# Two row blocks of the scores in one visit of TensorE, and a new order of the fill work

## The chip, the cores and the metric

The kernel runs on one core of a Trainium2 chip. The metric is the device time of one execution in microseconds (us); the kernel before was timed three times, and the median counts. The granted TensorE clock is 1.00 (2.4 GHz) throughout the profiled execution.

## The reference, cut to what matters

One decoder layer over 512 tokens and a width of 1024, in float32:

- RMS norm, then one input projection into two head groups: eight heads of block-sparse attention (MoBA) and four heads of differential attention, which have two maps of 64 dimensions and one value of 128.
- In both groups q and k get an RMS norm per head and rotary positions. With 512 tokens and MoBA blocks of 256 keys every past block is chosen, so MoBA attention is plain causal attention here.
- Differential attention subtracts lambda times the second softmax map from the first, multiplies by v, and norms each head's output.
- The output projection is added to the input; an RMS norm and a SwiGLU feed-forward part (hidden width 2816) follow, with another residual.

Attention is therefore, for every head and every query row, `softmax(mask(q k^T / 8)) v` over the causal keys.

## The kernel before

**Number format.** Large products are made of three TensorE matmuls in float32r: each operand is split into a rounded part ("hi", by ScalarE) and the remainder ("lo", by VectorE), and hi x hi, hi x lo and lo x hi are accumulated (lines 1473 to 1475 in the helper `product`). Small products (scores, transposes, mean squares, probabilities times v) are plain float32.

**Pairs.** Attention is worked through in eight pairs of maps: pairs 0 to 3 are MoBA (two heads each), pairs 4 to 7 differential (one head with its two maps each). A map takes 64 of the 128 partitions. For each pair three projections (q, k, v) of 8 steps each are needed, 24 "fills" of three matmuls; fill n of pair p+1 is issued between the attention steps of pair p, so that TensorE has work while VectorE and ScalarE handle the softmax of pair p. In pair 7 the fills are steps of the output projection. The first four fills of pair 1 come before the first scores.

**One pair on TensorE.** `scores(t, qt)`, qt = 0 to 3, multiplies the 128 queries of row block qt with the (qt+1) x 128 causal keys, for both maps, into PSUM banks 2 and 3. `turn_v` transposes v (bank 7). `turn_p(t, qt)` transposes the normed probabilities into banks 4 and 5. `mean_squares(t+1)` and `spread_k(t+1)` serve the norms of the next pair. `heads_out` multiplies with v in bank 6. `turn_o(t-1)` transposes the normed output of a differential head. The next scores need `k_ready`, which VectorE writes once `spread_k` is done.

**One row block on the other engines.** `maxima`: VectorE adds the mask to the diagonal block in PSUM (line 1011), takes the row maxima (1014) and makes the bias (1017). `exps`: ScalarE takes the exponentials of both maps with their sums (622). `norm`: VectorE inverts the sums (1027) and scales the probabilities of a MoBA pair (1030, 1031), or makes the factor of the second map (1033) and combines the maps (1036). `pt_copy`: ScalarE copies the transposed probabilities (632). Scores of row block qt+1 overwrite banks 2 and 3 and wait for the exponentials of block qt.

**Next pair's preparation.** ScalarE evacuates q, k and v (`q_evac`, `k_evac`, `v_evac`, lines 593, 596, 608). SP's queue rotates q and k by DMA (four of 64 KB each) and, between them, issues the loads of weight tiles (512 KB each). VectorE applies rotary positions (`q_rope`, `k_rope`, 974 to 978), computes the scales with eleven small dependent operations (`scales`, 919 to 929), spreads k's scale (965) and writes `k_ready` (1002). `project_hi` (ScalarE, 549) and `project_lo` (VectorE, 936) split weight tiles.

**A bank shared by q and v.** The projections of q and v go to bank 0, that of k to bank 1. The first fill of a pair's q therefore waits until v of the pair before has been copied out; v's copy waits for the last of the 24 fills:

```python
if j == 0 and from_(p, 1):
    pe.wait_ge(v_ev, p)
```

**What sets the order.** The order on every engine is written out by hand, in the texts of ScalarE (lines 676 to 757), VectorE (1107 to 1197) and TensorE (1655 to 1777), with separate texts for pair 0, pairs 1 to 3, pair 4, pairs 5 and 6, and pair 7. An engine takes its instructions in that order, and semaphores hold it where data aren't ready. After a differential pair, `o_squares`, `o_norm`, `turn_o`, `mix_hi` and `mix_lo` norm its output, during the pair that follows.

Of the kernel before, what the change touches and what calls it, by code (L numbers as in the profile page):

```python
# [58 lines left out]
WARM = 4  # L59

# [71 lines left out]
def build(nc, x, wt, vec, gain2, lams, ident_in, mask_in, cos_in, sin_in, out):  # L132
    with ExitStack() as ctx:
# [211 lines left out]

        def maps(moba):

            return range(2) if moba else range(1)
# [196 lines left out]
        def _(act):  # L545
# [64 lines left out]
            def exps(t, qt, moba):  # L610

                W = (qt + 1) * P
                act.wait_ge(nb_s, t * 4 + (qt + 1))
                for a in range(2):
                    i = 2 * qt + a

                    if qt >= 2:
                        act.wait_ge(pt_s, turned(t, qt - 2, a, moba))
                    elif from_(t, 1):
                        moba_before = t - 1 < MOBA_PAIRS if isinstance(t, int) else moba  # L620
                        act.wait_ge(pt_s, turned(t - 1, qt + 2, a, moba_before))
                    nc.scalar.activation(PR[qt % 2][:, a, 0:W], ps[:, 2 + a, 0:W], ACT.Exp, bias=NB[:, i:i + 1],  # L622
                                         scale=RQ[:, i:i + 1], accum_out=SUM[:, i:i + 1]).then_inc(ex_s, 1)

            def pt_copy(t, qt, moba):

                for a in maps(moba):
                    act.wait_ge(pt_s, turned(t, qt, a, moba))
                    if from_(t, 1):
                        act.wait_ge(pv_s, t)  # L630
                    bank = 4 + (a if moba else qt % 2)
                    nc.scalar.activation(PT[:, a, 0:qt + 1, qt * P:(qt + 1) * P],
                                         ps[:, bank, 0:(qt + 1) * P].rearrange("p (k q) -> p k q", q=P),
                                         ACT.Copy).then_inc(pt_ev, 1)
# [40 lines left out]

            exps(0, 0, True)
            project_hi(1, 2)
            exps(0, 1, True)
            pt_copy(0, 0, True)
            q_evac(1, False)  # L680
            pt_copy(0, 1, True)
            exps(0, 2, True)
            project_hi(1, 3)
            k_evac(1, False)
            exps(0, 3, True)
            pt_copy(0, 2, True)
            pt_copy(0, 3, True)
            v_evac(1)
            project_hi(1, 4)
            mix_hi(0, True)  # L690

            with act.Fori(1, MOBA_PAIRS) as t:
# [12 lines left out]
                project_hi(t + 1, 4)  # L705
                v_evac(t + 1)
                mix_hi(t, True)
# [4 lines left out]
            exps(4, 1, False)  # L712
            exps(4, 2, False)
            project_hi(5, 3)
            q_evac(5, False)
            pt_copy(4, 1, False)
            exps(4, 3, False)
            k_evac(5, False)
            pt_copy(4, 2, False)
            pt_copy(4, 3, False)  # L720
# [3 lines left out]
            with act.Fori(MOBA_PAIRS + 1, PAIRS - 1) as t:  # L724
                project_hi(t + 1, 2)
                exps(t, 0, False)
                pt_copy(t, 0, False)
                exps(t, 1, False)
                o_squares(t - 1)
                exps(t, 2, False)  # L730
                project_hi(t + 1, 3)
                q_evac(t + 1, True)
                pt_copy(t, 1, False)
                exps(t, 3, False)
                k_evac(t + 1, True)
                pt_copy(t, 2, False)
                mix_hi(t - 1, False)
                pt_copy(t, 3, False)
                project_hi(t + 1, 4)
                v_evac(t + 1)  # L740
# [3 lines left out]
            exps(7, 0, False)  # L744
            exps(7, 1, False)
            pt_copy(7, 0, False)
            exps(7, 2, False)
# [3 lines left out]
            exps(7, 3, False)  # L751
# [155 lines left out]
        def _(dve):  # L907
# [72 lines left out]
            def q_rope(p):  # L980
                if from_(p, 1):
                    dve.wait_ge(sc_s, p * 4)
# [14 lines left out]
            def k_norm(p):  # L997
                dve.wait_ge(kb_s, p + 1)
                dve.wait_ge(k_step, p * 3 + 3)
                if from_(p, 1):  # L1000
                    dve.wait_ge(sc_s, p * 4)
                nc.vector.tensor_tensor(KF[:], KS[:], ps[:, 7], ALU.mult).then_inc(kn_s, 1)

            def maxima(t, qt):

                W = (qt + 1) * P
                n = t * 4 + (qt + 1)
                i = slice(2 * qt, 2 * qt + 2)
                diagonal = ps[:, 2:4, qt * P:W]
# [4 lines left out]
                nc.vector.tensor_reduce(MX[:, i], ps[:, 2:4, 0:W], AX.X, ALU.max).then_inc(mx_s, 1)  # L1014
# [5 lines left out]
            def norm(t, qt, moba):  # L1020


                W = (qt + 1) * P
                i = 2 * qt
                p0, p1 = PR[qt % 2][:, 0, 0:W], PR[qt % 2][:, 1, 0:W]
                dve.wait_ge(ex_s, t * 8 + (i + 2))
                nc.vector.reciprocal(RS[:, i:i + 2], SUM[:, i:i + 2]).then_inc(rs_s, 1)
                dve.wait_ge(rs_s, t * 4 + (qt + 1))
                if moba:
                    nc.vector.tensor_scalar(p0, p0, RS[:, i:i + 1], None, ALU.mult).then_inc(pn_s, 1)  # L1030
                    nc.vector.tensor_scalar(p1, p1, RS[:, i + 1:i + 2], None, ALU.mult).then_inc(pn_s, 1)
                else:
                    nc.vector.scalar_tensor_tensor(out=NL[:, qt:qt + 1], in0=SUM[:, i:i + 1], scalar=MLAM,
                                                   in1=RS[:, i + 1:i + 2], op0=ALU.mult, op1=ALU.mult).then_inc(lr_s, 1)
                    dve.wait_ge(lr_s, t * 4 + (qt + 1 - 4 * MOBA_PAIRS))
                    nc.vector.scalar_tensor_tensor(out=p0, in0=p1, scalar=NL[:, qt:qt + 1], in1=p0,
                                                   op0=ALU.mult, op1=ALU.add).then_inc(pn_s, 1)
                    if qt == TT - 1:
                        sums = SUM.rearrange("p (t a) -> p t a", a=2)[:, :, 0]
                        nc.vector.scalar_tensor_tensor(out=EO, in0=sums, scalar=EPS, in1=sums, op0=ALU.mult,  # L1040
                                                       op1=ALU.mult).then_inc(eo_s, 1)
# [65 lines left out]
            maxima(0, 0)  # L1107
            norm(0, 0, True)
            maxima(0, 1)
            v_scale(0)  # L1110
            norm(0, 1, True)
            maxima(0, 2)
            project_lo(1, 2)
            norm(0, 2, True)
            maxima(0, 3)
            project_lo(1, 3)
            norm(0, 3, True)
# [7 lines left out]
            with dve.Fori(1, MOBA_PAIRS) as t:  # L1125
                maxima(t, 0)
                norm(t, 0, True)
                maxima(t, 1)
                v_scale(t)
                norm(t, 1, True)  # L1130
                maxima(t, 2)
                project_lo(t + 1, 2)
                norm(t, 2, True)
                maxima(t, 3)
                project_lo(t + 1, 3)
                norm(t, 3, True)
                q_rope(t + 1)
                scales(t + 1)
                k_rope(t + 1)
                k_norm(t + 1)  # L1140
                project_lo(t + 1, 4)
                mix_lo(t, True)

            maxima(4, 0)
            norm(4, 0, False)
# [837 lines left out]
```

## Time and profile before

| | us |
|---|---|
| median of three runs | 622.77 (622.37 to 623.19) |
| span of the profiled execution, first to last instruction | 619.5 |
| TensorE busy | 600.8 |
| VectorE busy | 483.7 |
| ScalarE busy | 311.4 |
| pairs 0 to 7, first scores to the end of the last heads | 36.52 to 255.30 |

For the profiled execution the profile gives the span; what lies around the span has no figure of its own there and is read from the median of the runs, 3.3 us above it. Matmuls overlap in their pipeline: one of 512 columns is shown with 0.39 us, and the next one starts 0.23 us after it. The start times are what counts for TensorE's pace. Idle time of an engine other than TensorE costs nothing unless TensorE waits for its result.

### The profile page before, as it was taken

Reading aid. Unit: us, or ns where it says so; the run is one execution under the profiler, and the core shown is the slowest. Engines: PE = TensorE matmul, PEld = TensorE weight load, DVE = VectorE, ACT = ScalarE, POOL = GpSimd, SP = SyncE. Lnnn points to the kernel's source line nnn. Section 1 sums busy time; section 2 is a strip of 40 time slices with the busy share of each in tenths; the row PEclk is TensorE's granted clock in tenths of the full one; section 3 lists DMA queues with packets and bytes.
Section 4 is the critical chain, followed back from the end, with each engine's and each line's share of the span. In section 5 each row is a group of like instructions: output and inputs, shape, how many; then the busy total and the mean of one; then the engine's idle time right before and its main releaser. Section 6 shows DMA issues by size and latency. Waiting matters only on the chain.

```text
span 619.5 us, 10404 instructions
## 1 busy us (share of the span) xinstructions
PE 600.8 (97%) x3774; PEld 515.5 (83%) x3774; DVE 483.7 (78%) x821; ACT 311.4 (50%) x533; POOL 28.1 (5%) x28
## 2 busy tenths in 40 slices
PE   5999999999999889999999999999999999999997
PEld 5867677776777576878999999999999998888886
DVE  3867777787687888678878787788778877999774
ACT  5445546364545454445653644445444555555551
POOL 0000000000000000000000000000000012145200
PEclk9999999999999999999999999999999999999999
DMA  8324040322314051512413422333213449699901
GB/s 306 92 70 129 1 136 17 119 59 77 102 35 137 0 169 68 170 36 95 178 35 136 137 71 85 119 136 130 75 69 136 136 125 260 196 190 204 198 35 68
DMA packets 32953, 70.31 MB, mean 114 GB/s; under 512 B 3344, under 2 KB 3728, under 8 KB 32912
## 3 DMA queue, kind: packets, MB, share of 16 engines
q1 hardware_dynamic: 26896, 58.22, 28.0%
q0 software_dynamic: 6016, 11.54, 10.6%
q8 instruction: 27, 0.44, 0.3%
q14 instruction: 14, 0.11, 0.1%
HBM read 63.45 MB, written 2.10 MB: 106 GB/s over the span
## 4 chain that ended last, share of the span: by engine, by line
PE 87%; DVE 7%; issue 2%; ACT 2%; DMA 1%; SPq 0%; DVEq 0%; ACTq 0%
PE ps L1473 26%; PE ps L1474 25%; PE ps L1475 25%; PE ps L1537 3%; PE ps L1550 2%; PE ps L1505 2%; PE ps L1567 1%; DMA w_raw<-wt 1%; DVE w_lo L954 1%; ACT probs L622 1%; PE ps L1575 1%; DVE w_lo L936 1%; PE ps L1796 1%; DVE residual L1205 0%; DVE small L1014 0%
## 5 line engine op out<-in xcount | busy, mean ns | idle before, releaser
L1473 PE MATMUL ps<-h_sum_parts,w_hi 128*128 128x256 f32 x432 | 120.6, 279 | 0.7 <-ACT q_kept L806 0.7
L1474 PE MATMUL ps<-h_sum_parts,w_hi 128*128 128x256 f32 x432 | 120.9, 280 | 0.0
L1475 PE MATMUL ps<-h_sum_parts,w_lo 128*128 128x256 f32 x432 | 120.5, 279 | 0.0
L1473 PE MATMUL ps<-h_parts,w_hi 128*128 128x512 f32 x192 | 81.2, 423 | 2.7 <-DVE h_parts L1071 2.4
L1473 PEld LDWEIGHTS ps<-h_sum_parts,w_hi 128*128 128x128 f32 x432 | 81.2, 188 | 0.9 <-ACT q_kept L806 0.9
L1474 PEld LDWEIGHTS ps<-h_sum_parts,w_hi 128*128 128x128 f32 x432 | 81.1, 188 | 0.0
L1475 PEld LDWEIGHTS ps<-h_sum_parts,w_lo 128*128 128x128 f32 x432 | 80.8, 187 | 0.0
L1475 PE MATMUL ps<-h_parts,w_lo 128*128 128x512 f32 x192 | 75.4, 393 | 0.0
L1474 PE MATMUL ps<-h_parts,w_hi 128*128 128x512 f32 x192 | 75.0, 391 | 0.0
L622 ACT ACTIVATE probs<-ps,small 128x128 f32<-128x128 f32 (+3 forms) x64 | 39.0, 614 | 51.8 <-DVE small L1017 51.8
L1473 PE MATMUL ps<-w_hi,hidden_parts 128*128 128x512 f32 x154 | 59.9, 389 | 0.0
L1475 PE MATMUL ps<-w_hi,hidden_parts 128*128 128x512 f32 x154 | 59.9, 389 | 0.0
L1474 PE MATMUL ps<-w_lo,hidden_parts 128*128 128x512 f32 x154 | 59.9, 389 | 0.0
L1474 PE MATMUL ps<-h_first_parts,w_hi 128*128 128x256 f32 x192 | 53.8, 280 | 0.0
L1473 PE MATMUL ps<-h_first_parts,w_hi 128*128 128x256 f32 x192 | 53.7, 280 | 0.0
L1475 PE MATMUL ps<-h_first_parts,w_lo 128*128 128x256 f32 x192 | 53.6, 279 | 0.0
L1473 PEld LDWEIGHTS ps<-h_parts,w_hi 128*128 128x128 f32 x192 | 36.2, 189 | 19.8 <-issue 13.7
L954 DVE TENSOR_TENSOR w_lo<-w_raw,w_hi 128x1024 fp32r<-128x1024 f32 x29 | 35.3, 1222 | 16.4 <-ACT w_hi L584 16.4
L1475 PEld LDWEIGHTS ps<-h_parts,w_lo 128*128 128x128 f32 x192 | 36.0, 188 | 8.2
L954 DVE TENSOR_TENSOR w_lo<-w_raw_odd,w_hi 128x1024 fp32r<-128x1024 f32 x25 | 30.5, 1221 | 13.2 <-ACT w_hi L584 13.2
L1474 PEld LDWEIGHTS ps<-h_parts,w_hi 128*128 128x128 f32 x192 | 36.2, 189 | 5.3
L529 POOL DMA_DIRECT2D w_raw_odd<-wt x12 | 14.6, 1214 | 541.3 <-DVE w_lo L1313 541.3
(175 smaller groups left out, 1248.7 us busy)
## 6 DMA issues: line engine op xcount, KB each, us to landing
w_raw<-wt SPq DMA_DIRECT2D x61, 512.0 KB, 4.2
w_raw_odd<-wt SPq DMA_DIRECT2D x24, 512.0 KB, 4.2
w_raw_odd<-wt POOLq DMA_DIRECT2D x12, 512.0 KB, 7.8
down_raw<-wt SPq DMA_DIRECT2D x6, 512.0 KB, 11.0
w_raw<-wt POOLq DMA_DIRECT2D x5, 512.0 KB, 10.2
residual<-x SPq DMA_DIRECT2D x4, 512.0 KB, 5.1
q_rotated<-q_gained SPq DMA_DIRECT2D x32, 64.0 KB, 2.0
k_rotated<-k_gained SPq DMA_DIRECT2D x32, 64.0 KB, 2.0
```

The lines of the kernel that those rows point to most:

```text
L529: pool.dma_start(down_raw("B11", c).rearrange("p (f n) -> p f n", n=SEQ), down_rows(role, c), accum_op=ALU.add).then_inc(tb_added[c], 16)
L622: nc.scalar.activation(PR[qt % 2][:, a, 0:W], ps[:, 2 + a, 0:W], ACT.Exp, bias=NB[:, i:i + 1], scale=RQ[:, i:i + 1], accum_out=SUM[:, i:i ...
L936: nc.vector.tensor_tensor(WL[:, slot], RAW[:, slot], WH[:, slot].bitcast(F32), ALU.subtract).then_inc(w_lo, 1)
L954: nc.vector.tensor_tensor(WL[:, n % SLOTS], product_source(n), WH[:, n % SLOTS].bitcast(F32), ALU.subtract).then_inc(c_lo, 1)
L1473: nc.tensor.matmul(dst, lh, rh, start=start, stop=False, skip_group_check=True)
L1474: nc.tensor.matmul(dst, lh, rl, start=False, stop=False, skip_group_check=True)
L1475: return nc.tensor.matmul(dst, ll, rh, start=False, stop=stop, skip_group_check=True)
L1505: ins = nc.tensor.matmul(ps[:, 7, c:c + 2], SQ[:, tt * P:(tt + 1) * P], IND, start=True, stop=True, skip_group_check=True)
L1537: ins = nc.tensor.matmul(ps[:, 2 + a, 0:W], QF[rows[a], qs], KF[rows[a], 0:W], start=True, stop=True, skip_group_check=True)
L1550: ins = nc.tensor.transpose(ps[:, bank, kt * P:(kt + 1) * P], PR[qt % 2][:, a, kt * P:(kt + 1) * P], ident[:])
L1567: ins = nc.tensor.matmul(ps[rows, 6, qs], VF[:, kt, rows], PT[:, a, kt, qs], start=kt == 0, stop=kt == TT - 1, skip_group_check=True)
L1575: ins = nc.tensor.matmul(ps[:, 6, qs], PT[:, 0, kt, qs], VF[:, kt], start=kt == 0, stop=kt == qt, skip_group_check=True)
```

## The change

Row blocks 0 and 1 become one visit: `VISITS = ((0, 1), (2,), (3,))`. TensorE writes the scores of block 1 (256 wide) at columns 0 to 255 of banks 2 and 3 and those of block 0 at columns 256 to 383, four matmul calls with one semaphore step. VectorE adds the mask to both diagonal blocks, which lie side by side, in one operation, takes two sets of maxima, and makes one bias for all four; ScalarE takes four exponentials; VectorE inverts four sums at once. The transposed probabilities of block 0 in a MoBA pair go to the last quarter of banks 4 and 5, so that blocks 0 and 1 can be turned one right after the other. `pt_copy` of block 0 in a MoBA pair waits for the turn of block 1.

The order of all three engines is new in every pair. On TensorE, with the fills as numbers (S scores, T turn_p, TV turn_v, TO turn_o, MS mean_squares, H0 and H1 heads_out, SK spread_k; the indices are row blocks):

```
pairs 1-3 before: 1 S0 2 TV 1 S1 T0 4 S2 4 T1 S3 6 T2 MS T3 5 H0 SK 1 H1
pairs 1-3 after:  1 S01 2 TV 4 S2 1 T0 T1 3 S3 T2 6 T3 MS 4 H0 SK H1 3
pair 0 before:    4 S0 TV 2 S1 3 T0 1 S2 1 T1 4 S3 2 T2 5 T3 MS 2 H0 SK H1
pair 0 after:     4 S01 2 TV 4 S2 1 T0 T1 3 S3 T2 3 T3 MS 4 H0 SK H1 3
pair 5, 6 before: 1 S0 1 TV 1 S1 T0 4 S2 4 T1 1 S3 1 TO 5 T2 1 MS T3 5 H0 SK H1
pair 5, 6 after:  1 S01 2 TV 4 S2 1 T0 T1 3 S3 2 T2 TO 4 T3 MS 4 H0 SK H1 3
pair 7 before:    TV 1 S0 3 S1 3 S2 2 T0 T1 2 S3 TO 5 T2 2 T3 3 H0 H1
pair 7 after:     S01 TV 5 S2 2 T0 T1 3 S3 3 T2 TO 4 T3 4 H0 H1
```

Pair 4 after is as pairs 5 and 6 without TO. The core of the diff, in which visit 1 is row block 2 and visit 2 is row block 3:

```diff
+VISITS = ((0, 1), (2,), (3,))
+NV = len(VISITS)
+def score_at(qt):
+    return 2 * P if qt == 0 else 0
...
-            def scores(t, qt):
+            def scores(t, v):
...
-                for a in range(2):
-                    ins = nc.tensor.matmul(ps[:, 2 + a, 0:W], QF[rows[a], qs], KF[rows[a], 0:W], start=True,
-                                           stop=True, skip_group_check=True)
+                for qt in VISITS[v]:
+                    W = (qt + 1) * P
+                    at = score_at(qt)
+                    for a in range(2):
+                        ins = nc.tensor.matmul(ps[:, 2 + a, at:at + W], QF[rows[a], qt * P:W], KF[rows[a], 0:W],
+                                               start=True, stop=True, skip_group_check=True)
                 ins.then_inc(sc_s, 1)
...
+                at = P if v == 0 else first * P
+                diagonal = ps[:, 2:4, at:at + blocks * P].rearrange("p a (b k) -> p a b k", b=blocks)
                 dve.wait_ge(sc_s, n)
-                nc.vector.tensor_tensor(diagonal, diagonal, mask[:].unsqueeze(1).broadcast_to([P, 2, P]),
+                nc.vector.tensor_tensor(diagonal, diagonal,
+                                        mask[:].unsqueeze(1).unsqueeze(1).broadcast_to([P, 2, blocks, P]),
                                         ALU.add).then_inc(masked, 1)
...
             def pt_copy(t, qt, moba):
...
-                    act.wait_ge(pt_s, turned(t, qt, a, moba))
+                    act.wait_ge(pt_s, turned(t, max(qt, 1) if moba else qt, a, moba))
...
             with act.Fori(1, MOBA_PAIRS) as t:
+                project_hi(t + 1, 2)
                 exps(t, 0, True)
                 pt_copy(t, 0, True)
                 exps(t, 1, True)
-                project_hi(t + 1, 2)
+                pt_copy(t, 1, True)
+                q_evac(t + 1, False)
                 project_hi(t + 1, 3)
                 exps(t, 2, True)
-                pt_copy(t, 1, True)
-                q_evac(t + 1, False)
-                exps(t, 3, True)
+                pt_copy(t, 2, True)
                 k_evac(t + 1, False)
-                pt_copy(t, 2, True)
                 pt_copy(t, 3, True)
                 project_hi(t + 1, 4)
+                mix_hi(t, True)
                 v_evac(t + 1)
-                mix_hi(t, True)
...
             with dve.Fori(MOBA_PAIRS + 1, PAIRS - 1) as t:
                 maxima(t, 0)
+                v_scale(t)
+                project_lo(t + 1, 2)
                 norm(t, 0, False)
                 maxima(t, 1)
-                v_scale(t)
-                project_lo(t + 1, 2)
+                o_norm(t - 1)
                 norm(t, 1, False)
                 maxima(t, 2)
-                o_norm(t - 1)
-                maxima(t, 3)
+                mix_lo(t - 1, False)
                 norm(t, 2, False)
-                norm(t, 3, False)
-                mix_lo(t - 1, False)
-                project_lo(t + 1, 3)
                 q_rope(t + 1)
                 scales(t + 1)
                 k_rope(t + 1)
+                project_lo(t + 1, 3)
                 k_norm(t + 1)
                 project_lo(t + 1, 4)
```

In pairs 5 and 6 ScalarE takes `o_squares(t - 1)` ahead of the first exponentials, and `q_evac` and `mix_hi(t - 1)` ahead of the last. In pair 7 ScalarE takes `out_hi` and `mix_hi(6)` ahead of the last exponentials, as before, and VectorE takes `o_norm(6)` between the second maxima and their norm. In the MoBA pairs VectorE takes `project_lo(t + 1, 4)` ahead of `k_norm(t + 1)`.

## Rows read from the trace of the kernel before

**Rows 1.** the page, busy time, share of the span and instructions.

```profile
PE 600.8 (97%) x3774; PEld 515.5 (83%) x3774; DVE 483.7 (78%) x821; ACT 311.4 (50%) x533; POOL 28.1 (5%) x28
```

**Rows 2.** busy time by stretch, from scores to scores; stretch, length, busy (instructions).

```profile
36.52:64.22 27.70, 26.07 (x141) 18.21 (x140) 20.14 (x49) 14.14 (x33) 0.00 (x0) 1.00 0.26 77
...
92.15:120.02 27.87, 27.87 (x150) 19.91 (x149) 20.64 (x49) 14.45 (x33) 0.00 (x0) 1.00 0.24 75
...
147.88:174.67 26.79, 26.33 (x144) 20.17 (x143) 20.37 (x50) 13.32 (x29) 0.00 (x0) 1.00 0.26 79
174.67:203.28 28.61, 27.05 (x147) 20.60 (x147) 22.80 (x63) 14.17 (x37) 0.00 (x0) 1.00 0.24 75
203.28:255.30 52.02, 49.08 (x261) 36.92 (x261) 41.97 (x107) 26.43 (x70) 0.00 (x0) 1.00 0.24 82
```

**Rows 3.** waits of TensorE from 36 to 256 us; total, times, longest.

```profile
PE ps L1537 <- ACT probs L622: 2.1, 5, 0.6
PE ps L1537 <- DVE k_ready L1002: 2.0, 2, 1.3
PE ps L1522 <- DVE k_ready L1002: 1.3, 1, 1.3
PE ps L1513 <- DVE k_rstd_spread L965: 0.5, 2, 0.3
PE ps L1550 <- DVE probs L1036: 0.4, 2, 0.2
```

**Rows 4.** TensorE's timeline, pair 2; start, length of the group, instructions.

```profile
92.15 0.49 PE L1537 MATMUL ps<-k_ready,q_ready 64*128 64x128 f32 x4
...
95.30 0.70 PE L1537 MATMUL ps<-k_ready,q_ready 64*128 64x256 f32 x4
...
103.31 1.13 PE L1537 MATMUL ps<-k_ready,q_ready 64*128 64x512 f32 x4
104.36 0.50 PE L1473 MATMUL ps<-h_parts,w_hi 128*128 128x512 f32 x1
104.70 0.39 PE L1474 MATMUL ps<-h_parts,w_hi 128*128 128x512 f32 x1
...
108.33 0.39 PE L1475 MATMUL ps<-h_parts,w_lo 128*128 128x512 f32 x1
```

**Rows 5.** TensorE's weight loads at the same 512-wide scores.

```profile
103.30 0.30 PEld L1537 LDWEIGHTS ps<-k_ready,q_ready 64*128 64x128 f32 x4 [0.17 <-ACT probs L622]
```

**Rows 6.** TensorE's timeline before pair 0, first fill of pair 1.

```profile
32.44 0.39 PE L1475 MATMUL ps<-h_parts,w_lo 128*128 128x512 f32 x1
...
33.61 0.47 PE L1473 MATMUL ps<-h_parts,w_hi 128*128 128x512 f32 x1 [0.34 <-ACT v_by_dim L608]
```

**Rows 7.** ScalarE's timeline, v's copy there; exponentials in pair 2.

```profile
32.87 0.60 ACT L608 ACTIVATE v_by_dim<-ps 128x512 f32<-128x512 f32 x1 [6.12 <-PE ps L1475]
...
94.14 0.46 ACT L622 ACTIVATE probs<-ps,small 128x128 f32<-128x128 f32 x1 [2.10 <-DVE small L1017]
...
97.51 0.56 ACT L622 ACTIVATE probs<-ps,small 128x256 f32<-128x256 f32 x1 [0.77 <-DVE small L1017]
```

**Rows 8.** VectorE's timeline, pair 2.

```profile
97.32 0.69 DVE L994 TENSOR_TENSOR v_turned<-ps,small 128x512 f32<-128x512 f32 x1
...
104.48 0.43 DVE L1011 TENSOR_TENSOR ps<-ps,mask 128x256 f32<-128x256 f32 x1 [0.42 <-PE ps L1537]
...
108.07 0.17 DVE L1027 RECIPROCAL small<-small 128x2 f32<-128x2 f32 x1 [0.53 <-ACT probs L622]
108.27 0.49 DVE L1030 TENSOR_SCALAR probs<-probs,small 128x512 f32<-128x512 f32 x1
```

**Rows 9.** VectorE's timeline, pair 5, output's norm and last combining.

```profile
184.08 0.16 DVE L921 SCALAR_TENSOR_TENSOR small<-small 128x4 f32<-128x4 f32 x1
...
186.48 0.69 DVE L1047 TENSOR_TENSOR o_normed<-ps,small 128x512 f32<-128x512 f32 x1
...
191.43 0.75 DVE L1036 SCALAR_TENSOR_TENSOR probs<-probs,small 128x512 f32<-128x512 f32 x1
```

More of the change, by code:

```diff
@@ L344, in turned, with turned_at @@
             return t * 4 + (4 * MOBA_PAIRS + qt + 1)
+        def turned_at(qt, moba):
+            return 3 * P if moba and qt == 0 else 0
         def maps(moba):
@@ L1018, in maxima @@
                                                op1=ALU.mult).then_inc(nb_s, 1)
[L1020 to L1041, printed above, removed]
@@ new lines, in norm @@
+            def norm(t, v, moba):
+                first, blocks = VISITS[v][0], len(VISITS[v])
+                i, last = 2 * first, 2 * (first + blocks)
+                dve.wait_ge(ex_s, t * 8 + last)
+                nc.vector.reciprocal(RS[:, i:last], SUM[:, i:last]).then_inc(rs_s, 1)
+                dve.wait_ge(rs_s, t * NV + (v + 1))
+                if not moba:
+                    nc.vector.scalar_tensor_tensor(out=NL[:, first:first + blocks], in0=SUM[:, i:last:2], scalar=MLAM,
+                                                   in1=RS[:, i + 1:last:2], op0=ALU.mult,
+                                                   op1=ALU.mult).then_inc(lr_s, 1)
+                    dve.wait_ge(lr_s, t * NV + (v + 1 - NV * MOBA_PAIRS))
+                for qt in VISITS[v]:
+                    W = (qt + 1) * P
+                    p0, p1 = PR[qt % 2][:, 0, 0:W], PR[qt % 2][:, 1, 0:W]
+                    if moba:
+                        nc.vector.tensor_scalar(p0, p0, RS[:, 2 * qt:2 * qt + 1], None, ALU.mult).then_inc(pn_s, 1)
+                        nc.vector.tensor_scalar(p1, p1, RS[:, 2 * qt + 1:2 * qt + 2], None,
+                                                ALU.mult).then_inc(pn_s, 1)
+                    else:
+                        nc.vector.scalar_tensor_tensor(out=p0, in0=p1, scalar=NL[:, qt:qt + 1], in1=p0, op0=ALU.mult,
+                                                       op1=ALU.add).then_inc(pn_s, 1)
+                if not moba and v == NV - 1:
+                    sums = SUM.rearrange("p (t a) -> p t a", a=2)[:, :, 0]
+                    nc.vector.scalar_tensor_tensor(out=EO, in0=sums, scalar=EPS, in1=sums, op0=ALU.mult,
+                                                   op1=ALU.mult).then_inc(eo_s, 1)
@@ L1107, in _ @@
             maxima(0, 0)
+            v_scale(0)
+            project_lo(1, 2)
             norm(0, 0, True)
             maxima(0, 1)
-            v_scale(0)
             norm(0, 1, True)
             maxima(0, 2)
-            project_lo(1, 2)
+            project_lo(1, 3)
             norm(0, 2, True)
-            maxima(0, 3)
-            project_lo(1, 3)
-            norm(0, 3, True)
             q_rope(1)
@@ L1157, in _ @@
             k_rope(5)
+            project_lo(5, 3)
             k_norm(5)
@@ L1177, in _ @@
                 k_rope(t + 1)
+                project_lo(t + 1, 3)
                 k_norm(t + 1)
@@ L1678, in _ @@
             heads_out(0, 1, True)
+            fill(3)
             with pe.Fori(1, MOBA_PAIRS) as t:
@@ L1727, in _ @@
             heads_out(4, 1, False)
+            fill(3)
             with pe.Fori(MOBA_PAIRS + 1, PAIRS - 1) as t:
@@ L1754, in _ @@
                 heads_out(t, 1, False)
+                fill(3)
             fill = out_filler()
+            scores(7, 0)
             turn_v(7)
-            fill(1)
-            scores(7, 0)
-            fill(3)
+            fill(5)
             scores(7, 1)
-            fill(3)
-            scores(7, 2)
             fill(2)
@@ L1766, in _ @@
             turn_p(7, 1, False)
-            fill(2)
-            scores(7, 3)
+            fill(3)
+            scores(7, 2)
+            fill(3)
+            turn_p(7, 2, False)
             turn_o(6)
-            fill(5)
-            turn_p(7, 2, False)
-            fill(2)
+            fill(4)
             turn_p(7, 3, False)
-            fill(3)
+            fill(4)
             heads_out(7, 0, False)
```

228 lines of the change are left out of this document (107 added, 121 removed).

## The prediction

> **What bounds the kernel now.** I read the page's busy times first. TensorE is busy 97% of the span [rows 1]: whatever the other engines save is worth only what it takes out of TensorE's waits. The stage table, cut at the first scores of each pair, says where there are any [rows 2]: pairs 1 to 3 have TensorE busy for their whole 27.9 us (pair 2 stands for them), pair 0 lacks 1.6 us, pair 4 0.5, pair 5 1.6, pairs 6 and 7 together 2.9. The waits of TensorE between 36 and 256 us add to 6.3 us, 2.1 of them on exponentials, 3.3 on k_ready, 0.5 on the k spread, 0.4 on normed probabilities [rows 3]. Start to start, against the pace of undisturbed neighbours, the same 15 stalls cost 8.0 us, since the pipeline also drains: 1.8 in pair 0, 0.6 in pair 4, 2.0 in pair 5, 3.7 in pairs 6 and 7. That is all the change can win from waits.
>
> The other reserve is the order of the stream itself. The 72 fill matmuls of a pair go at 0.227 to 0.229 us each (16 steps between the second and the eighteenth after the last scores take 3.63 us [rows 4]), 16.5 us in all. Every group of f32 work between them costs its own length, about 0.1 us ahead of it when it is scores or heads and 0.08 to 0.11 behind it (0.34 from 104.36 to 104.70 against 0.23 [rows 4]). What is left of pair 2's 27.87 [rows 2], 11.36 us, is the cost of its groups.
>
> **What the change removes from TensorE's stream.** No matmul goes away. Scores take, start to next start, 0.42, 0.63 and 1.06 us at 128, 256 and 512 wide (their rows less 0.07 us of tail [rows 4]): 0.21, plus 0.21 for every 128 columns, both heads side by side. The merged visit is 0.42 + 0.63 = 1.05 us if its halves only follow each other, 0.85 if the second has no 0.21 of its own; I take 0.95, as the weights of the second pass are loaded while the first runs (4 loads in 0.30 us at the head of a visit of 1.06 [rows 4, 5]), and keep 0.85 and 1.05 as bounds. One pair of edges (0.20) goes. The Trainium skill, "TensorE: Matmul & The Clock Gate", part 3 "The mechanism", says that a weight load overlaps matmuls in flight only where the row groups differ; the merged visit comes back to row group 0, so by that rule it is 1.05 and the sum 0.8 us higher. The trace is against the strict reading, by that row of loads, but shows no second visit behind a first.
> The other groups, start to next start in pairs 0 and 2 of TensorE's timeline less the fills' own pace: a turn appended to scores costs 0.09 us a transpose and no edge; turns of row blocks 0 and 1 together, six transposes like turn 2 of pair 0, 0.66; turn 3 and the mean squares 2.66; heads, k spread, heads in one piece 3.24. So a MoBA pair's groups cost 11.0 us, 0.37 less than now; pair 0 saves 0.36, pair 4 0.21, pairs 5 and 6 0.28 each, pair 7 0.4. Together -2.7 us.
>
> **What it adds: the wait for v_by_dim.** Now heads (and in MoBA pairs one fill) stand between the last v product of a pair and the first fill of the next, which writes the same bank 0 and waits for ScalarE's copy of v. After, each pair ends with three fills and the loop begins with fill(1), so nothing stands between them. The trace has this wait once with only a short k spread inside: last matmul 32.44, copy 32.87 for 0.60, next fill 33.61 [rows 6, 7]. That is 1.17 us instead of 0.23, plus 0.08 behind it: 1.0 us (0.9 to 1.05 with the spread of such wake-ups). Behind it on TensorE queue the fill, then the scores, so the whole stream moves. It comes at six pair ends, 0 to 5 (pair 6 is followed by scores, not by a fill): +6.0 us. Its cover today is the 0.8 us of heads; now mixed_parts covers nothing of it, being released before the three fills.
>
> **The new schedule, from the start of the merged scores (0).** VectorE: mask from 1.07; 512 elements per partition in PSUM step 0.61 (the v scaling, 0.69 with its overlap [rows 8]) to 0.86 (two masks of 0.43), I take 0.7; maxima 0.4 and 0.7; bias out at 3.1. ScalarE from 3.2: 0.45 + 0.45 + 0.56 + 0.69 (the rows for 128 and 256 wide, the last with its reading of the sum and the way to TensorE [rows 7]), so the second scores may start at 5.35. TensorE arrives there after fill 2, turn v, fill 4 at 5.70: margin 0.35, no wait. The project_lo and v scaling now between maxima and norm lie beside the exponentials (end 4.9, norm from 5.33): free. Turn 0 at 7.3 finds its probabilities (6.6). Second scores end 6.55, bias 8.1, exponentials 8.33 to 9.8; ScalarE's first copies of turned probabilities, which now wait for turn 1 too, end 8.3, just in time. Third scores arrive at 10.1 in MoBA pairs (margin 0.3), at 9.83 in differential ones (margin 0.04).
> The last step is where margin runs out. From the start of the 512-wide scores to their first normed map is 5.45 us and 0.1 to TensorE (103.31; mask 104.48; exponentials; reciprocal 108.07; scaling 108.27 for 0.49 [rows 4, 8]). Pairs 1 to 3 put turn 2 and six fills between (5.8 us): hidden. Pair 0 puts three (3.8): +1.7 us. Differential pairs put two fills, turn 2 and four fills: 5.65, against 6.0 with their extra small scale (0.25) and a combining operation of 0.75 instead of 0.49 [rows 9]: pair 4 +0.4. In pairs 5 and 6 the output's norm now sits between the second maxima and norm 1: 2.2 us of small steps and 0.6 (184.08 to 186.48 with a hiccup of 0.2, then the product [rows 9]); maxima 2 start at 12.1 instead of 11.0 and turn 3 finds its map at 17.0 where TensorE is at 15.85: +1.1 each. Pair 7: no fill before turn v and five behind it, so the second scores wait 0.4; turn 3 is ready 17.8, as ScalarE must first take mixed_parts behind turn o, against 16.9: +0.9; the fill that needs w_out_parts 0.1. Together +1.7 +0.4 +2.2 +1.4 = +5.7 us.
> DMAs: the moved evacuations issue the q and k rotations and the weight loads behind them on SP's queue. q is evacuated at 11.6 and needed at 16.6, k at 16.8 and needed at 22.0, loads are needed 5 us or more after their issue: hidden. k_ready, which ends 1.5 to 3 us before the scores that want it, stops being a wait even behind the project_lo now ahead of it in MoBA pairs; what is late next is v_by_dim, in every pair. After pair 7 the stream of w_out is TensorE's and moves one for one.
>
> **The sum.** Waits removed -8.0, groups -2.7, v_by_dim +6.0, new waits +5.7: +1.0 us. Walking the same schedule start by start gives +0.4 (pair 0 +0.4, pairs 1 to 3 +0.5 each, pair 4 +0.6, pair 5 -0.1, pairs 6 and 7 -1.95; the lower value of each edge taken). I take +0.8. The profiled execution spans 619.5 us, and 3.3 us lie between that and the median of 622.77; the change touches nothing outside the span, so 620.3 and **623.5**. Bounds: merged scores 0.1 each way in 8 pairs, 0.8; v wait -0.6 to +0.3; the waits behind the third scores 0.2 each in five pairs, 1.0. These hardly all fall together: 622.0 to 625.0.
>
> **Rivals.**
> (a) *The first chain binds everywhere.* Slower. Second scores have 0.35 us of margin behind mask, two maxima, bias and four exponentials. If the merged mask with its two broadcast axes costs 0.86, 0.16 goes; should the four-dimensional access be slower still, or the exponentials queue behind ScalarE's weight split, which now runs first in the pair, every 0.1 us beyond the margin costs 0.8 us over eight pairs, and the third scores, with 0.04 in differential pairs, follow at once. 0.6 us more of chain: +0.25 x 8 = 2.0, 625.5. For it: thin margins in all pairs. Against: TensorE's chains in the trace repeat within 0.05 us, and the split ends before 0. It decides from 0.35 us.
> (b) *The new waits are at their cheap end.* v copy 0.9, merged scores 0.85, and the last map ready 0.2 sooner five times: -0.6 -0.8 -1.0 = -2.4 from the forecast, 621.1, faster than before. For it: waits of the trace vary by 0.3 between pairs. Against: three terms must lean one way; the v wait is fixed by a copy that lasts 0.60 in all eight pairs.
> (c) *The visit isn't merged in effect.* Second halves wait for the first to drain: 1.05 and edges kept, +0.3 a pair, part swallowed by later waits: +1.5, 625.0. The row of loads is against it.
> A measurement of this kernel tells about 0.2% (1.2 us) from no change. Forecast 0.62 for itself, of which a third of its upper part passes 624.0; (a) 0.13, (b) 0.15, (c) 0.10. Faster by over 0.2% takes most of (b): 0.14. Slower takes (a), (c) and 0.12 of the forecast: 0.34. Same: 0.52. The range takes the forecast's own 622.0 to 625.0 and reaches a little into (a) and (b): 621.7 to 625.2.
>
> **What would show it.** In the changed trace: scores 0.85 to 1.05 from the first matmul of the merged visit to the next fill; no wait on k_ready; a wait of TensorE's fill line on v_by_dim six times, about 0.75 us idle each; waits on normed probabilities in pairs 0, 4, 5, 6 and 7 and none in 1 to 3; MoBA pairs of 28.4 to 28.5 us instead of 27.9; TensorE's busy time some 2 us less by overlap counted. I am wrong if the fill line shows no wait on v_by_dim, if scores wait on exponentials in pairs 1 to 3, or if pairs 6 and 7 together don't fall by 1.5 us or more.

## The result: 0.8% slower, and the profile after

The changed kernel took 627.15 us (median of 6 runs, 624.81 to 628.19) against 622.31 for the kernel before (6 runs, 620.69 to 623.19): ratio 1.0084, 95% interval 1.0069 to 1.0099. The forecast was 623.5 and its range ended at 625.2. The profiled execution took 626.56 us and spans 624.7 us; in the six runs 1.75 to 1.86 us lie outside the span. The kernel before's profiled 619.5 us therefore stood for some 621.3 us.

First the page of the changed kernel: the busy time of TensorE, and the granted clock in 40 slices.

```profile
PE 603.6 (97%) x3774; PEld 518.1 (83%) x3774; DVE 478.3 (77%) x793; ACT 309.3 (50%) x533; POOL 28.1 (4%) x28
...
PEclk9997999999999999999999999999999999999999
```

TensorE is as full as before [rows 1], but one slice, from 47 to 62 us, has a clock of 7 tenths. The kernel before has a 9 in all forty. Next, TensorE's waits of the changed kernel from 36 to 262 us (total, times, longest), which answer to [rows 3].

```profile
PE ps L1485 <- ACT v_by_dim L622: 4.7, 6, 0.8
PE ps L1566 <- DVE probs L1058: 2.8, 4, 0.9
PE ps L1566 <- ACT probsT L649: 1.5, 1, 1.5
PE ps L1550 <- ACT probs L638: 0.2, 1, 0.2
```

k_ready and the k spread are gone from the list, and the three waits named in the forecast stand in it: v_by_dim six times, normed probabilities in pairs 4 to 7 (written at line 1058 of the changed kernel), and the wait of pair 0 before turn 3, 1.5 us, which the trace puts down to ScalarE's copy of the third row block's turned probabilities. VectorE finishes the first normed map at 51.67 us, some 0.06 us before turn 3 starts, so the map that the forecast named was hardly earlier than that copy:

```profile
51.19 0.48 DVE L1054 TENSOR_SCALAR probs<-probs,small 128x512 f32<-128x512 f32 x1
```

Then the stretches of the changed kernel from scores to scores, answering to [rows 2] (stretch, length, busy time of the engines, granted clock, DMA share, GB/s).

```profile
36.15:67.53 31.38, 29.11 (x140) 20.52 (x139) 20.07 (x46) 14.08 (x33) 0.00 (x0) 0.89 0.22 68
...
96.08:124.63 28.55, 27.77 (x149) 19.86 (x149) 19.98 (x46) 14.10 (x33) 0.00 (x0) 1.00 0.24 73
...
153.18:180.58 27.40, 26.39 (x143) 20.05 (x142) 19.52 (x45) 12.40 (x30) 0.00 (x0) 1.00 0.26 77
180.58:210.65 30.07, 28.40 (x147) 21.65 (x147) 22.63 (x58) 13.85 (x38) 0.00 (x0) 0.94 0.24 71
210.65:260.60 49.95, 48.08 (x262) 36.70 (x261) 40.18 (x98) 26.73 (x71) 0.00 (x0) 1.00 0.29 89
```

| pairs | before | walked in the forecast | after | clock after |
|---|---|---|---|---|
| 0 | 27.70 | 28.1 | 31.38 | 0.89 |
| 1 to 3, each | 27.87 to 27.93 | 28.4 | 28.55 | 1.00 |
| 4 | 26.79 | 27.4 | 27.40 | 1.00 |
| 5 | 28.61 | 28.5 | 30.07 | 0.94 |
| 6 and 7 | 52.02 | 50.1 | 49.95 | 1.00 |

Where the clock is 1.00 the walk start by start (the forecast's second way of adding) holds within 0.15 us a pair. The two pairs where it is off, by 3.3 and 1.6 us, are the two with a clock below 1. The same changed kernel in steps of 2 us, around turn 3 of pair 0 and of pair 5:

```profile
50.00:52.00 2.00, 0.51 (x4) 0.27 (x3) 1.40 (x5) 2.00 (x7) 0.00 (x0) 1.00 0.63 135
52.00:54.00 2.00, 2.00 (x19) 2.00 (x17) 1.97 (x4) 1.92 (x5) 0.00 (x0) 0.88 0.53 201
54.00:56.00 2.00, 2.00 (x9) 1.90 (x9) 0.57 (x4) 0.89 (x1) 0.00 (x0) 0.50 0.26 62
56.00:58.00 2.00, 2.00 (x6) 1.52 (x6) 1.73 (x10) 0.00 (x0) 0.00 (x0) 0.50 0.60 139
58.00:60.00 2.00, 2.00 (x7) 1.51 (x5) 1.97 (x6) 0.00 (x0) 0.00 (x0) 0.50 0.99 365
60.00:62.00 2.00, 2.00 (x10) 0.49 (x8) 1.19 (x2) 0.00 (x0) 0.00 (x0) 0.91 0.21 86
...
196.00:198.00 2.00, 1.11 (x8) 0.69 (x7) 1.72 (x5) 1.63 (x5) 0.00 (x0) 1.00 0.47 176
...
200.00:202.00 2.00, 2.00 (x7) 1.57 (x6) 1.66 (x11) 0.66 (x1) 0.00 (x0) 0.57 0.31 74
202.00:204.00 2.00, 2.00 (x7) 1.57 (x6) 1.93 (x6) 0.00 (x0) 0.00 (x0) 0.57 0.80 260
```

0.50 is the lower level, 1.2 GHz. Summed over the rows it lasts 6.8 us in pair 0 and 3.4 us in pair 5, and costs half of that, 5.1 us. Each begins two to three microseconds after the end of a wait for the last map (the rows with 0.51 us busy of 2 and 1.11 of 2 hold these waits), in or behind the mean squares. What the matmuls look like there is in TensorE's timeline of the changed kernel, where the ordinary fills are left out and one slow fill is shown (start, length, instructions).

```profile
47.29 0.88 PE L1566 MATMUL ps<-ident,probs 128*128 128x128 f32 x6
...
51.73 1.09 PE L1566 MATMUL ps<-ident,probs 128*128 128x128 f32 x8 [1.49 <-ACT probsT L649]
52.66 0.95 PE L1517 MATMUL ps<-small,q_squared 128*128 128x2 f32 x8
53.47 1.82 PE L1517 MATMUL ps<-small,k_squared 128*128 128x2 f32 x8
...
56.58 0.63 PE L1485 MATMUL ps<-h_parts,w_hi 128*128 128x512 f32 x1
57.00 0.63 PE L1486 MATMUL ps<-h_parts,w_hi 128*128 128x512 f32 x1
```

The last two start 0.42 us apart instead of 0.23. The runs' own clocks tell the same: 624.81 us at 0.994, 626.4 and 626.6 at 0.991, 627.8, 628.0 and 628.2 at 0.989, 1.6 us for each 3.4 us at 1.2 GHz. At full clock this kernel would take about 621.4 us (an estimate, 626.56 less 5.1; no run of it had full clock). The kernel before, in the runs beside the experiments, takes 620.6 to 622.3 us at 1.00 (mostly under 621.5) and 621.9 to 623.4 at 0.997. So between the two profiled executions, whose spans differ by 5.2 us, the clock takes 5.1 and the schedule of the pairs 0.6; 0.4 comes back ahead of the pairs. Between the medians (4.8 us) it is some 0.7 of schedule and 4 of clock, since the median of the kernel before had one such stretch itself.

### The profile page after: what moved, and what is told of

It is laid out like the page before. It is cut to its first block, busy times and chain, and to the rows that moved or that the text cites. A ratio compares the mean times of both kernels' runs of the same rounds, so it can differ in the third digit from the quotient of the medians.

```text
span 624.7 us, 10337 instructions
## 1 busy us (share of the span) xinstructions
PE 603.6 (97%) x3774; PEld 518.1 (83%) x3774; DVE 478.3 (77%) x793; ACT 309.3 (50%) x533; POOL 28.1 (4%) x28
## 4 chain that ended last, share of the span: by engine, by line
PE 90%; DVE 4%; ACT 3%; issue 1%; DMA 1%; SPq 0%; ACTq 0%
PE ps L1485 27%; PE ps L1487 25%; PE ps L1486 25%; PE ps L1550 4%; PE ps L1517 2%; PE ps L1566 2%; PE ps L1583 2%; PE ps L1591 1%; ACT probs L638 1%; DMA w_raw<-wt 1%; DVE w_lo L966 1%; ACT v_by_dim L622 1%; PE ps L1802 1%; PE ps L1525 1%; DVE small L1030 1%
## 5 line engine op out<-in xcount | busy, mean ns | idle before, releaser
L1485 PE MATMUL ps<-h_parts,w_hi 128*128 128x512 f32 x192 | 82.7, 431 | 7.4 <-ACT v_by_dim L622 5.0
L1487 PE MATMUL ps<-h_parts,w_lo 128*128 128x512 f32 x192 | 76.9, 401 | 0.0
L1486 PE MATMUL ps<-h_parts,w_hi 128*128 128x512 f32 x192 | 76.5, 398 | 0.0
L1485 PEld LDWEIGHTS ps<-h_parts,w_hi 128*128 128x128 f32 x192 | 37.0, 193 | 25.5 <-issue 19.6
L638 ACT ACTIVATE probs<-ps,small 128x128 f32<-128x128 f32 (+3 forms) x64 | 38.9, 615 | 28.1 <-DVE small L1035 28.1
L1486 PEld LDWEIGHTS ps<-h_parts,w_hi 128*128 128x128 f32 x192 | 37.2, 194 | 5.8
```

The source lines that it names most:

```text
L638: nc.scalar.activation(PR[qt % 2][:, a, 0:W], ps[:, 2 + a, at:at + W], ACT.Exp, bias=NB[:, i:i + 1], scale=RQ[:, i:i + 1], accum_out=SUM[: ...
L1485: nc.tensor.matmul(dst, lh, rh, start=start, stop=False, skip_group_check=True)
L1486: nc.tensor.matmul(dst, lh, rl, start=False, stop=False, skip_group_check=True)
L1487: return nc.tensor.matmul(dst, ll, rh, start=False, stop=stop, skip_group_check=True)
```

## The experiments

All runs of one group stood on one chip beside the kernel before, whose medians were 622.24 (first four), 621.35 (second four) and 621.32 (last four). "Stretches" are 3.4 us at 1.2 GHz, estimated from a run's mean clock (half of 3.4 us is 0.27% of 625: 0.997 is one, 0.994 two, 0.991 three, 0.989 four). Where they lie is known for the one profiled run of each kernel only.

**The v waits hidden.** In pairs 0 to 6:

```diff
+fill(3)
 heads_out(t, 0, True)
 spread_k(t + 1)
 heads_out(t, 1, True)
-fill(3)
...
+v_evac(t + 1)
 mix_hi(t, True)
-v_evac(t + 1)
```

> The three fills at each pair's end stand ahead of the heads instead of behind them (pairs 0 to 6), and v is copied ahead of mixed_parts. Theory A (the schedule cost 0.8 us over the kernel before, of it six v waits of 1.0; the rest of the loss is the clock at 1.2 GHz for a stretch in pair 0 and one in pair 5): the v waits go, 5 to 6 us less than the changed kernel, the clock still falls in pair 0; about 621 us. Rival B (the v wait only moves on: the next scores then wait for k_ready, since less stands behind the k spread): 0 to 2 us less, waits on k_ready in its place.

Measured: 619.12 us (5 runs), ratio to before 0.9951 (0.9932 to 0.9970). One run at 0.999 took 615.59, four at 0.994 took 618.7 to 619.5. The profile shows no wait on v_by_dim in the pairs, nor on k_ready in its place: 5.8 us less than the estimate for the changed kernel at full clock (621.4). Rival B is out. The stretches went from three or four in most runs to two in four runs of five. The one profiled had none, though its waits for the last map stand with mean squares right behind (1.49 us in pair 0, 0.87 in pairs 5 and 6): theory A's fall in pair 0 didn't come in this run, and where the others had theirs isn't shown.

**Pair 0 fed.**

```diff
 turn_p(0, 2, True)
-fill(3)
+fill(6)
 turn_p(0, 3, True)
 mean_squares(1)
-fill(4)
+fill(1)
```

> Pair 0 alone: six fills instead of three ahead of turn 3, one instead of four behind the mean squares. Theory A (the clock falls where TensorE has stood waiting for the last map and then goes into transposes and mean squares): no wait, clock 1.00 all through pair 0, pair 0 of 28 us or less instead of 31.4; the changed kernel less 3.3 for the clock and 1 to 1.7 for the wait, some of it returned as a wait on the k spread: 4 us less. Rival C (the clock falls by chance of the chip or by the pattern of the whole pair, not by this wait): 1.7 us less at most, clock still at half in pair 0.

Measured: 623.25 us (10 runs), ratio 1.0021 (1.0004 to 1.0038); one to three stretches. The profile has full clock in pair 0 and the low stretches in pairs 4 and 5 (164 to 172 and 196 to 204 us). That pair 0 is at full clock is as theory A has it, and the median is 3.5 us under the changed kernel's 626.72 (measured again below; forecast 4). But in pair 4 TensorE had waited only 0.23 us for the last map (turn 3 at 164.68) before the clock fell at 167.2: the length of the wait alone doesn't decide.

**Pair 0, mean squares set apart.** The wait stays; `fill(2)` stands between `turn_p(0, 3)` and `mean_squares(1)`, and two behind.

> Pair 0 alone: the wait ahead of turn 3 stays, but two of the four fills that follow the mean squares stand between turn 3 and the mean squares. Theory A1 (wait and thin matmuls behind it together bring the clock down): the clock stays at 1.00, 3.3 us less than the changed kernel. Theory A2 (the 1.5 us of waiting alone brings it down): clock at half as before, time as the changed kernel. If neither the wait nor the thin matmuls matter (rival C): as the changed kernel too, and the run with six fills tells it from A2.

Measured: 624.65 us (8 runs), ratio 1.0039 (1.0022 to 1.0056), one to three stretches (most often two). The profile has the full 1.49 us of waiting in pair 0 and full clock there, low stretches in pairs 5 and 6, where the mean squares still stand right behind waits of 0.9 us. That speaks for A1, for one pair in one profile.

**The kernel before, starved.** In its pair 0 `fill(1)` between turns 2 and 3 and `fill(6)` behind the mean squares, for 5 and 2.

> The kernel before, pair 0 alone: one fill instead of five between turns 2 and 3, six instead of two behind the mean squares, so that TensorE waits some 1.5 us for the last map as in the changed kernel, with no merged visit anywhere. Theory A: the clock falls in pair 0 here too and costs 3.3 us; with the wait of 1.6 and less k_ready wait (-1.3) about 3 to 4 us more than before, 626. Rival C (only the new pattern brings the clock down): clock 1.00, 0 to 0.5 us more than before.

Measured: 622.65 us (10 runs), ratio 1.0021 (1.0003 to 1.0038). TensorE waits 1.46 us before turn 3, mean squares right behind, and the clock in pair 0 stays at 1.00 in the profile (its one low stretch is at 12 to 20 us):

```profile
55.01 1.09 PE L1550 MATMUL ps<-ident,probs 128*128 128x128 f32 x8 [1.46 <-ACT probsT L632]
```

```profile
54.00:58.00 4.00, 2.99 (x26) 2.94 (x27) 3.11 (x7) 2.08 (x6) 0.00 (x0) 1.00 0.65 186
```

Two runs of ten had no stretch, seven had one, one had three. Theory A missed here: a wait and thin matmuls behind it are not always enough.

**All maps fed.** Pair 0 as above, and

```diff
 # pairs 5 and 6 (pairs 4 and 7: fill(4) -> fill(5), one less behind)
 turn_o(t - 1)
-fill(4)
+fill(6)
 turn_p(t, 3, False)
 mean_squares(t + 1)
-fill(4)
+fill(2)
```

> The changed kernel with more fills ahead of turn 3: six instead of three in pair 0, five instead of four in pairs 4 and 7, six instead of four in pairs 5 and 6, and as many fewer behind; the v waits stay. Theory A (time is the schedule's sum plus 1.7 us for each 3.4 us stretch at 1.2 GHz, and such stretches come where TensorE waits for the last map and then goes into the thin mean squares): waits of 4.5 us go and the stretches in pairs 0, 4, 5 and 6 with them: 617 us, clock 1.00 or 0.997. Rival D (the v waits bring the clock down as well): clock still 0.994 to 0.991, 620 us or more.

Measured: 620.22 us (10 runs), ratio 0.9976 (0.9964 to 0.9989): three runs at full clock with 618.6 to 619.3, seven at 0.997. Rival D is out: six waits of 0.8 us stand at the pair ends as before (five put down to v_by_dim, the one behind pair 4 to w_lo), and in the profile the clock holds at all of them. Whether the one stretch of the other seven runs lies in the pairs or at the start (see below) isn't shown. The saving of the schedule is 2.8 us where 4.5 were expected: new waits come up behind the maps, 0.55 us for w_out_parts, 0.35 for the k spread and 0.15 ahead of the scores of pair 7; the other 0.6 or so isn't accounted for.

**Both repairs.** The v waits hidden and all maps fed.

> The fills ahead of turn 3 as in the run with all maps fed, and the last three fills of each pair ahead of the heads, v copied ahead of mixed_parts. Theory A: both savings add, 611 to 612 us at clock 1.00. Rival B (with the fills gone from behind the k spread, k_ready or the k spread is waited for): 613 to 616 us with those waits in the profile.

Measured: 611.80 us (4 runs, 611.66 to 613.30), ratio 0.9850 (0.9830 to 0.9871). This beats both kernels. Its stretches from scores to scores:

```profile
36.27:61.76 25.49, 25.49 (x141) 18.25 (x140) 19.44 (x46) 13.41 (x33) 0.00 (x0) 1.00 0.27 83
89.30:116.84 27.54, 27.54 (x150) 19.95 (x149) 20.07 (x46) 14.09 (x34) 0.00 (x0) 1.00 0.25 76
144.38:170.28 25.90, 25.90 (x143) 20.21 (x142) 19.97 (x46) 13.79 (x34) 0.00 (x0) 1.00 0.23 64
170.28:196.63 26.35, 26.35 (x147) 20.69 (x147) 22.10 (x59) 14.10 (x39) 0.00 (x0) 1.00 0.26 79
196.63:245.90 49.27, 48.08 (x262) 37.06 (x261) 40.86 (x99) 26.32 (x67) 0.00 (x0) 1.00 0.31 100
```

Length and TensorE's busy time are one number in pairs 0 to 5. Together, the merged visit, the new order and the two repairs take 9.2 us out of the pairs against [rows 2]; this run doesn't say how much of it is the merging. Pairs 1 to 3 last 27.54 us instead of 27.9.

**Mean squares apart in all four pairs.** As in pair 0 above, also in pairs 4, 5 and 6. No wait is taken away.

> The changed kernel with two of its fills moved from behind the mean squares to between turn 3 and the mean squares, in pairs 0, 4, 5 and 6; no wait is taken away. Theory A1 (a wait and the thin matmuls close behind it must come together for the clock to fall): schedule time as the changed kernel's at full clock, 621 to 622 us, clock 1.00 or 0.997. Theory A2 (the waits alone do it): clock 0.991 to 0.989 and 626 to 628 us, as the changed kernel.

Measured: 624.09 us (10 runs), ratio 1.0039 (1.0027 to 1.0051); four runs at full clock (622.6 to 623.1), six at 0.997. TensorE's waits over the whole execution, and the steps around pair 0's and pair 5's mean squares:

```profile
PE ps L1485 <- ACT v_by_dim L622: 5.0, 7, 0.8
...
PE ps L1566 <- DVE probs L1058: 2.8, 4, 0.9
...
PE ps L1566 <- ACT probsT L649: 1.5, 1, 1.5
```

```profile
54.00:56.00 2.00, 2.00 (x19) 1.92 (x17) 0.32 (x1) 1.02 (x2) 0.00 (x0) 1.00 0.27 66
...
58.00:60.00 2.00, 2.00 (x14) 0.85 (x12) 1.90 (x7) 0.00 (x0) 0.00 (x0) 1.00 0.96 360
...
200.00:202.00 2.00, 1.99 (x19) 1.80 (x18) 1.83 (x8) 0.00 (x0) 0.00 (x0) 1.00 0.20 76
```

The changed kernel has the same three waits to the tenth over its whole execution (the seventh wait on v_by_dim is ahead of pair 0), and here not one run of ten is below 0.997, where the changed kernel had none of ten above 0.994. This is the clearest of the runs: these waits, with two fills ahead of the mean squares, don't bring the clock down. Theory A1 expected 621 to 622 us at full clock and it is 622.6 to 623.1, some 1.4 over the estimate for the changed kernel: two more edges between fills and mean squares in each of four pairs.

**Both repairs, visits split again.** `VISITS = ((0,), (1,), (2,), (3,))`, with `scores(t, 1)` behind turn v and one fill (three in pair 7).

> The run with both repairs, but with row blocks 0 and 1 as two visits again (one or three fills and the turn of v between them), everything else in the same order. This prices the merging alone: two more edges (0.2 us) and 0.21 us of a visit's start in each pair, 0.4 x 8 = 3.3 us more than with both repairs if the merged halves run side by side; 1.6 us if only the edges count; 0 if the merging never mattered. VectorE and ScalarE have one more mask, bias and reciprocal each pair, and no wait on them is expected.

Measured: 623.50 us (7 runs), ratio 1.0026 (1.0013 to 1.0039); at full clock 621.63, 9.9 more than with both repairs. Expected were 3.3 at most. The order didn't fit four visits: TensorE waits 1.5 us for probabilities, 1.3 for exponentials, 0.6 for k_ready, and 1.6 us in two stalls that the trace puts down to no engine. Only pairs 1 to 3 compare: 28.15 us (93.07 to 121.22) against 27.54, 0.6 more a pair, of which some 0.2 is a later start of the last scores (0.54 us after the fill ahead of them, where 0.32 is usual). The 0.4 that is left agrees with the two halves running side by side. What the merging is worth in the other pairs stays open.

This profile also has a fall that theory A1 doesn't cover. Pair 7 has no mean squares. Its last map is waited for 1.45 us, four transposes follow, then a second wait of 0.55, then fills, and the clock falls at about 253.3 us:

```profile
251.90 0.66 PE L1581 MATMUL ps<-ident,probs 128*128 128x128 f32 x4 [1.45 <-DVE probs L1063]
253.11 0.62 PE L1500 MATMUL ps<-w_out_parts,mixed_parts 128*128 128x512 f32 x1 [0.55 <-DVE w_out_parts L962]
```

**The changed kernel again.**

> The changed kernel once more, beside the others, for how often and where its clock falls. Theory A: 0.994 to 0.989, two to four stretches of 3.4 us at 1.2 GHz, each within 3 us behind a wait for the last map, one of them in pair 0; 621.4 us plus 1.7 for each. Rival C (chance): another number of stretches, at places without such a wait.

Measured: 626.72 us (4 runs), ratio 1.0092 (1.0069 to 1.0115), three or four stretches. Low clock in pairs 0, 5 and 6 (52 to 60, 196 to 204, 228 to 236 us), each behind its wait for the last map.

**Fed in pairs 4 to 7 only.**

> The changed kernel with maps fed in pairs 4 to 7 as in the run with all maps fed, and pair 0 left as it is. Theory A: the stretches of pairs 4 to 6 go, those of pair 0 stay: 618.7 (all maps fed, full clock) plus 1.4 for the wait plus one or two stretches of 1.7, clock 0.997 to 0.994, so 622 to 623.5 us, the low clock in pair 0 alone. Rival C: no clear place.

Measured: 622.81 us (10 runs), ratio 1.0016 (0.9999 to 1.0032); eight runs with two stretches, one with one, one at full clock. The profile has one in pair 0 (52 to 60 us) and one at 12 to 20 us, ahead of all pairs; pairs 4 to 7 are at full clock, as theory A has it.

**The kernel before, dense.** In its pair 0 turn 2 right behind the last scores, then `fill(3)`, turn 3, mean squares, `fill(6)`.

> The kernel before, pair 0 alone: turn 2 right behind the last scores, three fills, the wait for the last map, turn 3, mean squares, six fills, so the thin f32 matmuls stand on both sides of the wait as in the changed kernel; no merged visit. Theory A1 (wait and thin matmuls within a few us bring the clock down, whatever kernel they stand in): a low stretch in pair 0, clock 0.997 to 0.994 over what the kernel before shows, 624 us. If pair 0 stays at full clock, as it did with turn 2 and a fill ahead of the wait: what brings the clock down in the changed kernel's pair 0 needs something more than these, and 622 us.

Measured: 626.35 us (6 runs), ratio 1.0075 (1.0049 to 1.0100), one to four stretches. TensorE's timeline of this kernel (fills left out), then its steps of 2 us:

```profile
49.15 1.13 PE L1537 MATMUL ps<-k_ready,q_ready 64*128 64x512 f32 x4
50.21 0.88 PE L1550 MATMUL ps<-ident,probs 128*128 128x128 f32 x6
...
55.29 1.44 PE L1550 MATMUL ps<-ident,probs 128*128 128x128 f32 x8 [2.12 <-ACT probsT L632]
56.52 1.71 PE L1505 MATMUL ps<-small,q_squared 128*128 128x2 f32 x8
```

```profile
52.00:54.00 2.00, 1.17 (x6) 0.61 (x4) 1.31 (x3) 2.00 (x5) 0.00 (x0) 1.00 0.01 4
54.00:56.00 2.00, 0.71 (x6) 0.71 (x7) 1.42 (x4) 1.29 (x5) 0.00 (x0) 0.97 0.40 98
56.00:58.00 2.00, 2.00 (x12) 2.00 (x10) 1.52 (x3) 1.17 (x2) 0.00 (x0) 0.50 0.81 256
58.00:60.00 2.00, 2.00 (x11) 2.00 (x11) 0.03 (x1) 0.00 (x0) 0.00 (x0) 0.50 0.67 238
```

The fall of pair 0 in a kernel with no merged visit, made by moving four of its fills: 0, 3 and 6 stand ahead of turn 2, ahead of turn 3 and behind the mean squares, where 2, 5 and 2 stood. The wait is 2.1 us here, not 1.5, so the dense order and the longer wait aren't told apart. The clock falls at 55.9 us, in the transposes of turn 3 and before the first mean square (56.52), so here the mean squares didn't bring on the fall.

**v waits hidden, mean squares apart.**

> The run with the v waits hidden, and besides two fills between turn 3 and the mean squares in pairs 0, 4, 5 and 6; the waits for the last map stay. Theory A1: schedule as with the v waits hidden, 615.6 us at full clock, plus 0.5 for four more edges, and no low stretch in pairs 0, 4, 5, 6 where the run without this had two: 616 to 617 us. Theory A2 (waits alone): 619 us as without it.

Measured: 617.81 us (4 runs), ratio 0.9935 (0.9912 to 0.9957): 616.45 at full clock, 617.7 to 618.1 at 0.997. The profiled run's one low stretch is the one at 12 to 20 us. A1 again.

**All profiles counted.** Take every wait of 0.8 us or more for the last map in pairs 0, 5 and 6. With the mean squares right behind turn 3, the clock fell within 3.2 us after the wait in 10 of 16; with two fills between them, in 0 of 7. In the 12 cases where these maps were fed instead and no wait stood, it never fell. So the pattern makes a fall likely and not certain.

## Why the prediction was wrong

- **The sum of the schedule held.** Taking 5.1 us of low clock off the changed kernel's pairs, 224.45 us become 219.35, 0.6 more than 218.8 before; forecast +0.8 (+0.4 and +1.0 by the two ways of adding). The groups' saving of 0.37 us in a MoBA pair was right too: 27.54 us in pairs 1 to 3 without the v wait, 0.32 to 0.39 less than before. None of the prediction's own signs of being wrong came. A slip without effect on the sum: the working speaks of 15 stalls where [rows 3] has 12. TensorE's busy time rose, 600.8 to 603.6, where some 2 us less were expected, because matmuls last longer at 1.2 GHz (0.63 us instead of 0.39).
- **The v wait** was right in place, number and size: six times, last matmul at 65.50, next at 66.67. Hiding it gave 5.8 us, forecast 6.0.
- **The waits for the last map** were right in place: pair 0 1.5 (forecast 1.7), pair 4 0.2 (0.4), pairs 5 and 6 0.9 each (1.1), pair 7 0.8 (0.9); pairs 1 to 3 none. Pair 7's first wait was 0.2 (0.4).
- **The merged visit** takes 0.85 us from its start to the next fill (36.15 to 37.00), the lower bound. The rule of the Trainium skill that the prediction cites, that a weight load overlaps matmuls only in other row groups, would have given 1.05, and the trace doesn't bear it out here; rival (c) is out with it, and so is (a): second scores wait nowhere in pairs 0 to 6.
- **The step that failed** is the price of the new waits: "Pair 0 puts three (3.8): +1.7 us" and "+1.1 each". I priced them at the time TensorE stands still and put the clock at nothing, because it was 1.00 all through the profiled execution. In pairs 0, 5 and 6 (which of them varies from run to run) TensorE's clock often falls behind such a wait, to 1.2 GHz for 3.4 or 6.8 us: two to four such stretches in the ten runs of the changed kernel, 3.3 to 6.6 us, 5.1 in the profiled one. Feeding the maps, or two fills between turn 3 and the mean squares, left none or one. No rival had it. The Trainium skill, "TensorE: Matmul & The Clock Gate", part 1 "HAM oscillation — how this bites in real kernels", describes a kernel whose matmul bursts are each followed by a DMA wait longer than the burst, and which loses the clock every time. The trace agrees in kind only: here the clock fell behind waits of 0.2 to 2.1 us in a stream that is 97% busy, and not every time.
- **Reading the base** was a second, small error. I put 3.3 us between span and time; it is 1.8. The rest, 1.5 us, agrees with one low stretch in the median's run that the profiled one hadn't: the clocks of those first three runs aren't on record, but nearly all later runs of the kernel before at 622.2 us and more have 0.997. With 1.8 the forecast would have been 622.1 us, 0.7 above the estimate for a run at full clock and further from the measured median.

What stays open is what brings the clock down in one case and not in the next. Behind the same 1.49 us in pair 0 it fell in three of four profiles with the changed kernel's pair 0, and behind 1.46 us in the starved kernel before it didn't, in one profile. It fell once behind 0.23 us, and twice with no mean square ahead of the fall. The runs leave the dense order (turn 2 close ahead of the wait), the length of the wait and chance from run to run as candidates.

## What to carry to other kernels

A wait of TensorE can be dearer than its length where transposes, mean squares or other thin matmuls follow it: here 1.5 us of waiting cost up to 3.4 us more in clock. Where a wait can't be removed, try wide matmuls between the thin ones behind it; two fills between turn 3 and the mean squares, with every wait kept, were worth 2.6 us (626.72 to 624.09). One profile at full clock doesn't show that the clock is safe: look at the mean clock of every run. And before work is put last in a loop, ask what the loop's first instruction waits for: three fills on the wrong side of the heads cost 6 us; on the right side, with v copied first, they gave, with the merged visit and fed maps, 1.5%.

## What the runs showed of the hardware

- A kernel's time goes with its mean granted clock from run to run, with nothing changed in it: 620.6 to 622.3 us for the kernel before at 1.00 (mostly under 621.5), and 621.9 to 623.4 at 0.997.
- A low stretch at 12 to 20 us, ahead of all pairs, stands in the five profiles in which TensorE's first product waited 3.0 to 3.4 us for h_parts (the starved and the dense kernel before, both repairs split, fed in pairs 4 to 7, v hidden with mean squares apart), and in none of the nine where it waited 1.8 to 2.6. Two of the five are the kernel before with only its pair 0 changed, so it can presumably lose 1.7 us (half of 3.4) before attention begins; its own profile doesn't show it.
- Two pairs of matmuls on row groups 0 and 64, 128 and 256 wide, take 0.85 us one behind the other, where each pair alone takes 0.42 and 0.63: the second has no start of its own.
